# Activation transposes moved from TensorE to transposing DMAs in a decoder layer, and one projection folded into another

## The reference

```python
xn = rms_norm(h, norm_mix)
h = h + (g_a * (o_a @ w_br_gla) + g_b * (o_b @ w_br_dil)) @ w_mix_out
p = softmax(einsum('bshd,bmhd->bhsm', q, k) * X_HEAD_DIM ** -0.5)
h = h + einsum('bhsm,bmhd->bshd', p, v).reshape(b, s, D_MODEL) @ w_xo
```

## Time and profile before

| | us |
|---|---|
| median of 3 runs | 3063.55 (3058.01 to 3063.57) |
| profiled execution | 3062.74 |
| its span on the slowest core (the others from 3043.2) | 3061.2 |
| PE busy | 2918.9 |
| VectorE busy | 1843.2 |
| ScalarE busy | 1296.6 |
| GpSimd busy | 953.5 |

### The profile page before, as it was taken

The page is one execution under the profiler, slowest core; times in us unless marked ns, Lnnn a source line. Parts: engine busy times, 40 slices in busy tenths (PEclk is TensorE's granted clock), DMA queues, the critical chain, the costliest instruction groups (busy, mean ns, idle before and its releaser), DMA issues.

```text
span 3061.2 us, 55019 instructions; the slowest of 8 cores (3043.2 to 3061.2 us)
## 1 busy us (share of the span) xinstructions
PE 2918.9 (95%) x17454; PEld 1461.5 (48%) x17454; DVE 1843.2 (60%) x2994; ACT 1296.6 (42%) x2524; POOL 953.5 (31%) x1442
## 2 busy tenths in 40 slices
PE   5999999999999999899999989998999999999998
PEld 2444544555666554444444434444444444444443
DVE  4877766677766787344544346666644744754753
ACT  3666665566655666322232245665211211211211
POOL 1433333666776777233333210000200100100100
PEclk9999999999999999999999999999999999999999
DMA  6221103211221423644757395446811011011010
GB/s 145 72 73 50 55 28 80 61 50 40 55 65 43 100 78 84 138 132 150 188 147 167 107 192 176 159 148 193 165 56 64 20 56 69 15 55 69 15 55 28
DMA packets 96609, 278.99 MB, mean 91 GB/s; under 512 B 10920, under 2 KB 12228, under 8 KB 92868
## 3 DMA queue, kind: packets, MB, share of 16 engines
q1 hardware_dynamic: 81648, 223.91, 21.6%
q0 software_dynamic: 13568, 50.96, 10.8%
q10 hardware_dynamic: 1108, 0.60, 0.1%
HBM read 223.70 MB, written 102.63 MB: 107 GB/s over the span
## 4 chain that ended last, share of the span: by engine, by line
PE 78%; DVE 7%; ACT 6%; issue 5%; DMA 4%; DVEq 0%; ACTq 0%; POOL 0%; SPq 0%; POOLq 0%
PE psum L245 75%; PE psum L249 3%; ACT jh L271 1%; DMA wdn<-w_dn 1%; ACT junkX L271 1%; DVE on_112 L304 1%; ACT L271 1%; DMA x2i_220<-xn_d 0%; DMA oat<-oaT_d 0%; DVE cm_71 L308 0%; DMA h1x_234<-h_d 0%; DMA wvr_137<-w_gvr 0%; DMA grow_135<-gvec 0%; DVE x3s_246 L314 0%; DMA h1x_236<-h_d 0%
## 5 line engine op out<-in xcount | busy, mean ns | idle before, releaser
L245 PE MATMUL psum<-wd_140,xnT 128*128 128x512 bf16 x768 | 184.2, 385 | 7.8 <-DMA wd_140<-w_dil 7.8
L314 POOL COPY hist<-abt_278 128x2 f32<-128x2 f32 x88 | 17.4, 197 | 556.0 <-ACT abt_278 L313 556.0
L245 PE MATMUL psum<-wd_174,xnT 128*128 128x512 bf16 x768 | 185.4, 384 | 0.0
L245 PE MATMUL psum<-wd_175,xnT 128*128 128x512 bf16 x768 | 182.1, 380 | 0.0
L313 ACT COPY abt_278<-psum 128x512 f32<-128x512 f32 x88 | 50.2, 570 | 243.5 <-PE psum L245 243.5
L271 ACT ACTIVATE gl_276<-cv_0_272 128x512 f32<-128x512 f32 x88 | 55.5, 631 | 217.6 <-DVE cv_0_272 L304 217.6
L271 ACT ACTIVATE gl_277<-cv_1_273 128x512 f32<-128x512 f32 x88 | 55.5, 631 | 216.0 <-DVE cv_1_273 L304 216.0
L278 DVE TENSOR_TENSOR mab_197<-psum,sig_196 128x512 f32<-128x512 f32 x64 | 44.2, 691 | 146.2 <-PE psum L245 142.0
L245 PEld LDWEIGHTS psum<-wd_174,xnT 128*128 128x128 bf16 x768 | 103.0, 146 | 48.0
L278 DVE TENSOR_TENSOR qg_145<-psum,gqk 128x512 f32<-128x512 f32 x96 | 66.2, 689 | 90.0 <-ACT sq_142 L271 58.1
L278 DVE TENSOR_TENSOR qg_144<-psum,gqk 128x512 f32<-128x512 f32 x96 | 66.2, 690 | 89.1 <-ACT sq_142 L271 82.1
(11 more groups left out here) (748 smaller groups left out, 7821.0 us busy)
## 6 DMA issues: line engine op xcount, KB each, us to landing
ogl_176<-og_d SPq DMA_DIRECT2D x96, 260.0 KB, 4.9
og_d<-og_170 SPq DMA_DIRECT2D x32, 260.0 KB, 2.1
og_d<-og_171 SPq DMA_DIRECT2D x32, 260.0 KB, 2.1
og_d<-og_172 SPq DMA_DIRECT2D x32, 260.0 KB, 2.1
oaT_d<-oT_113 SPq DMA_DIRECT2D x32, 256.0 KB, 2.0
oat<-oaT_d SPq DMA_DIRECT2D x32, 256.0 KB, 4.3
xtT_203<-x SPq DMA_DIRECT2D x16, 512.0 KB, 7.3
h_d<-xtT_203 SPq DMA_DIRECT2D x16, 512.0 KB, 6.0
```

The costliest lines, as they stand in the source:

```text
L245: return self._add("pe", lambda e: e.matmul(o, l, r, start=start, stop=stop), [lhsT, rhs], [out], xr=xr)
L314: return self._add(eng, lambda e: e.tensor_copy(o, i), [in_], [out])
```

## The change

Transposing DMAs on SP (`dmat`, a new helper) take the place of `trans8` in `ntrans` from tile 8 on, `R_t`, `trans`, `og_trans`, `x2trans`, `q_trans` and `n_trans`. The keys of GLA, the memory and the first 8 input tiles stay on TensorE.

- The input tile is stored to DRAM (`xs_d`), and when a slab's four tiles are there, eight DMAs bring it back transposed, one for each 128 channels, each with a buffer record of its own. VectorE multiplies the gain in before (`gmb`, a broadcast load).
- The FFN's input is stored as it is, and four transposing loads bring a slab back (`x3_load`). The gain of the cross-attention's norm goes into the weights `wxq` on GpSimd (`kv_gx`).
- Orders move: in the GLA loop the values and scores of the next chunk come before `R_r`, and `P_za`, `P_z` after it; `trans` comes one step after the projections instead of two; `score`, `outp` and `x_out` come one iteration later, and the loop has one iteration more. `qkT` has four buffers. The copy of `va` goes from VectorE to ScalarE. Three slab loads wait for the last transpose of the dilated stage.
- The memory's values are made transposed (`kv_v`), multiplied once with the output projection (`kv_mx`, 32 matmuls), and `outp` is only a product of the probabilities with the inverse denominator; `x_out` multiplies them with the merged matrix.

```diff
+    def dmat(self, out, in_, xr=()):
+        o, i = out.ap, in_.ap
+        return self._add("sp", lambda e: e.dma_start_transpose(out=o, in_=i), [in_], [out], dma=True, xr=xr)
...
+            fw.stt("dve", xs[:, :], c["xt"][:, :], c["ss"][:, 2:3], gmb[:, :], ALU.mult, ALU.mult)
...
+        fw.dma(V(xs_d[i], xs_d[i].t[i * 128:(i + 1) * 128, :]), TCx[i]["xs"][:, :])
+        if i % 4 == 3:
...
+            for kc in range(8):
+                cs_ = slice(kc * 128, (kc + 1) * 128)
+                fw.dmat(V(xnk[s_][kc], xn[s_].t[:, kc, :]), V(xs_d[i - 3], xs_d[i].t[rows_, cs_]),
+                        xr=[V(xs_d[i - q], xs_d[i].t[rows_, cs_]) for q in range(3)])
...
     def R_t(c):
-        pt = trans8(PB.next(), cst_[c]["on"])
         oT = oTr.next()
-        fw.copy("act", oT[:, :, :], pt)
+        fw.dmat(oT[:, :, :], cst_[c]["on"][:, :])
         fw.dma(V(oaT_d[c], oaT_d[c].t[c]).rearrange("p (c t) -> p c t", c=8), oT[:, :, :])
...
-        pt = trans8(ptr_p, c["qkb"][:, :, :].rearrange("p a d -> p (a d)"))
         qkT = CC["qkTr"].next()
-        fw.copy("act", qkT[:, :, :], pt)
+        c["dT"] = fw.dmat(qkT[:, :, :], c["qkb"][:, :, :].rearrange("p a d -> p (a d)"))
...
         R_o(c)
-        if nx and c4 == 0:
-            P_za(s_ + 1)
         if nx:
             for h in ((), (0,), (1, 2), (3,))[c4]:
                 P_qk(s_ + 1, h)
         if c + 1 < NT:
-            R_r(c + 1)
-        if nx and c4 == 0:
-            P_z(s_ + 1)
+            R_v(c + 1, 0)
+            R_v(c + 1, 1)
+        if c + 1 < NT:
+            R_a(c + 1)
         if i < NT:
             nscale(i)
+            ntrans(i)
...
         R_on(c)
+        R_t(c)
...
         if c + 1 < NT:
-            R_v(c + 1, 0)
-            R_a(c + 1)
-            R_v(c + 1, 1)
+            R_r(c + 1)
+        if nx and c4 == 0:
+            P_za(s_ + 1)
+            P_z(s_ + 1)
...
+    def og_trans(i):
+        fw.dmat(ogc["obts"][i // 4 % 2][i % 4][:, :, :], TA[i]["obn"][:, :])
...
-        i, j, k = step, step - 2, step - 3
+        i, j, k = step, step - 1, step - 3
...
+    def kv_mx(h):
+        for mb in range(2):
+            for half in range(2):
+                cs_ = slice(half * 512, (half + 1) * 512)
+                p_ = PB.next()
+                for dc in range(2):
+                    fw.mm(p_[:, :], KV["VT"][:, 2 * h + dc, mb * 128:(mb + 1) * 128], KV["wxo"][h][:, dc, cs_],
+                          start=(dc == 0), stop=(dc == 1))
+                fw.copy("act", KV["MX"][h][:, mb, cs_], p_[:, :])
...
-        pt = trans8(PB.next(), qn)
-        fw.copy("dve", V(qTsub[s_ % 2][t_], qTs[s_ % 2].t[:, :, t_ * 128:(t_ + 1) * 128]), pt)
+        fw.dmat(qTsub[i // 4 % 2][i % 4][:, :, :], TC[i]["qn"][:, :])
...
+        fw.tt("dve", XL["pn"][s_ % 2][h][:, :, :], SC[s_][h][:, :, :], SC[s_]["rd"][:, :].raw(0, [[0, 2], [1, 512]]), ALU.mult)
...
+    def x3_load(s_):
+        for t_ in range(4):
+            i = s_ * 4 + t_
+            fw.dmat(F_["x3s"][t_][:, :, :], V(x3_d[i], x3_d[i].t[i]))
```

More of the change, by code:

```diff
@@ L509, in xn_reg @@
         for q in range(4):
-            xn[4 * hf + q] = b.sub("xn%d" % (4 * hf + q), xn_h[:, hf, :, q * 512:(q + 1) * 512])
+            s_ = 4 * hf + q
+            xn[s_] = b.sub("xn%d" % s_, xn_h[:, hf, :, q * 512:(q + 1) * 512])
+            if s_ >= 2:
+                xnk[s_] = [xn[s_]] + [b.sub("xn%d_%d" % (s_, kc), xn[s_].t) for kc in range(1, 8)]
+            else:
+                xnk[s_] = [xn[s_]] * 8
     xn_reg(0)
@@ L1081, in og_alloc @@
         ogc["ogl"] = r_.ring("ogl", 1, (128, 3, 520), F32)
-        ogc["obt"] = [r_.sb("obt%d" % q, (128, 4, 512), BF16) for q in range(2)]
+        ogc["obt"] = [r_.sb("obt%d" % q, (128, 4, 4, 128), BF16) for q in range(2)]
+        ogc["obts"] = [[b.sub("obt", b.t[:, t_]) for t_ in range(4)] for b in ogc["obt"]]
         ogc["rc"] = r_.ring("rcb", 2, (128, 8), F32)
@@ L1112, in og_div @@
         TA[i]["obn"] = obn
-    def og_trans(i, bank):
-        s_, t_ = i // 4, i % 4
-        ptb = bank[:, :].bitcast(BF16)
-        for cc in range(4):
-            fw.tr(ptb[:, cc * 128:(cc + 1) * 128], TA[i]["obn"][:, cc * 128:(cc + 1) * 128], ident_b)
-        obt = ogc["obt"][s_ % len(ogc["obt"])]
-        fw.copy("act", obt[:, :, t_ * 128:(t_ + 1) * 128], ptb[:, 0:512].rearrange("p (c t) -> p c t", c=4))
+    def og_trans(i):
+        fw.dmat(ogc["obts"][i // 4 % 2][i % 4][:, :, :], TA[i]["obn"][:, :])
     def oat_load(s_):
@@ L1153, in merge_br @@
             for kc in range(4):
-                fw.mm(py[:, :], sl[:, 16 + kc, :], ogc["obt"][s_ % 2][:, kc, :], start=(kc == 0), stop=(kc == 3))
+                ap = ogc["obt"][s_ % 2].t[:, :, kc, :]
+                ob = [V(b, ap) for b in ogc["obts"][s_ % 2]]
+                fw.mm(py[:, :], sl[:, 16 + kc, :], ob[0], start=(kc == 0), stop=(kc == 3), xr=ob[1:])
         ma = T1["ma"][br].next()
@@ L1208, in c_step @@
         if 0 <= t_ - 1 < 8 and ph == 1:
-            og_trans(t_ - 1, pj.next())
+            og_trans(t_ - 1)
         if 0 <= t_ < 8 and ph == 2:
@@ L1292, in kv_mm, with kv_v @@
         return p_
-    def kv_v(m):
-        for half in range(2):
-            p_ = kv_mm(m, half, True)
-            fw.copy("act", KV["Vm"][:, m, half * 512:(half + 1) * 512], p_[:, :])
+    def kv_v(q):
+        for c2 in range(2):
+            p_ = P.next()
+            for j in range(2):
+                c = q * 4 + c2 * 2 + j
+                for kc in range(8):
+                    fw.mm(p_[:, j * 256:(j + 1) * 256], KV["w"][:, kc, c * 128:(c + 1) * 128], KV["mn"][:, kc, :],
+                          start=(kc == 0), stop=(kc == 7))
+            c = q * 4 + c2 * 2
+            fw.copy("act", KV["VT"][:, c:c + 2, :], p_[:, :].rearrange("p (j n) -> p j n", j=2))
     def kv_k(m):
@@ L1329, in build @@
                (6, 1): [lambda: kv_v(1)], (6, 2): [kv_wxq]}
+    for q_ in range(4):
+        kv_plan[(7, q_)] = [lambda q_=q_: kv_gx(q_)]
     for s_ in range(NS):
@@ L1343, in build @@
                     if m > 0:
-                        og_trans(i - 1, P.next())
+                        og_trans(i - 1)
                 else:
@@ L1359, in build @@
             if 0 < s_ < NS - 1 and m == 7:
-                og_trans((s_ + 1) * 4 + 3, P.next())
+                og_trans((s_ + 1) * 4 + 3)
             for f_ in kv_plan.get((s_, m), ()):
@@ L1572, in build @@
     kv_wxo()
-    for k in range(NT + 11):
-        bg()
+    for k in range(NT + 12):
+        bg(2)
+        if 5 <= k < 9:
+            kv_mx(k - 5)
         if k < 5:
@@ L1579, in build @@
                 mix(NT - 4 + k)
-            x2trans(NT - 5 + k, PB.next())
+            x2trans(NT - 5 + k)
         if k == 5:
@@ L1620, in build @@
         if k >= NT + 5:
-            for _ in range(1 if k < NT + 9 else 2):
+            for _ in range(1 if k < NT + 10 else 2):
                 cur = up(0, len(UPD))
```

190 lines of the change are left out of this document (97 added, 93 removed).

## The result

The changed kernel takes 3137.59 us (median of four runs, 3135.5 to 3145.8) against 3062.85 for the kernel before: a ratio of 1.0252, 95% interval 1.0231 to 1.0274. The profiled execution has a span of 3134.0 us on its slowest core, 72.8 more than before. The forecast was 2998.

The account below looks back on a forecast made before the run. TensorE, busy 95%, was taken to bound the kernel. Gains of 43.2 (dilated), 5.8 (GLA) and 39.8 (cross-attention) less 23.8 (merge) took 65 us off 3062.7, giving 2998 us; range 2915 to 3045.

Parts of the forecast that it names:

- What left TensorE: Whole kernel: 2112 transposes (118.8 us) and a net 20.7 us of merged matmuls leave TensorE, 139.5 us if all stays hidden.
- X: Landing time of a 256 KB transposing DMA: bounded between 2.0 and 4.3 us, taken as 3.
- o: Spacing of the eight 128 KB slices replacing a group of input transposes: 0.32 to 4.1 us, taken as 1.15.
- upper bound of 130 ns a packet: Queue-line price per packet, giving 4.1 us as the upper end of the slice spacing.
- transposes are the bound: Rival: each 256 B piece costs a mean packet, 8.3 us per transpose; about 3460 us, cross-attention +90; chance 0.11.
- Dilated: Dilated stage, 96 items: DMA transposes stay hidden under 9.2 us of cover, each item 0.45 us shorter, gain 43.2 us.
- GLA: GLA stage: 25.1 us of transposes and 22.1 of waits go, six stalls behind slices add 41.4; net -5.8 us.
- The 22.1 us of waits on `on` and `vs`: GLA stage: PE's waits on `on` (12.0) and `vs` (10.1) go through the new order.
- Merge: Merge stage: 19.4 us of transposes go, six slab-boundary waits of 6.5 us plus 1.5 per restart add 43.2; net +23.8.
- Cross-attention: Cross-attention: 31.1 us of transposes and 20.7 of matmuls go, 12 given back where DMA is full; 8.2 us iterations, net -39.8.
- The rest: FFN input loads, slab loads, `wxq` scaling, constants and gain broadcast: covered or within the prologue, 0 us.
- 0.84 for faster: Chance of a faster kernel: 0.46 both stalls, 0.30 all or most hidden, 0.08 larger stalls.

Follow-up runs that it names:

- experiment 2: Changed kernel with input tiles from tile 8 transposed one by one from SBUF, no DRAM trip or slices: 3093.8 us on cores 0 to 3, against 3128.0.
- experiment 8: Changed kernel with all input-tile transposes back on TensorE, `R_t` still by DMA: 3098.9 to 3104.5 us, ratio 1.0129 to the kernel before.
- Experiment 1: Changed kernel with a slab's last dilated-output transpose issued ahead of that step's loads and store on SP: 3090.5 us on cores 0 to 3, against 3128.0.
- Experiment 3: Changed kernel with cross-attention's denominators after the query projection and query statistics before the residual's: 3107.7 us on cores 0 to 3, against 3128.0.
- experiment 5: Changed kernel with four extra, overwritten 512-column matmuls in each of 32 query projections: 3133.0 to 3137.7 us, ratio 1.0247 to the kernel before.
- experiment 4: Changed kernel with 13 `w_up` loads in cross-attention each waiting for its own iteration's query projection: 3102.7 us on cores 0 to 3, against 3128.0.
- experiment 7: Changed kernel with the last five mixer output norm tiles' transposes back on TensorE: 3111.3 to 3117.8 us, ratio 1.0170 to the kernel before.
- experiment 12: Changed kernel with edits of experiments 1 to 4, plus GLA's last four `R_t`, last five norm and first eight query transposes on TensorE: ratio 0.9778 to kernel before.
- experiment 6: Kernel before with only the dilated q/k transposes moved to DMA, one step after the projections, four buffers: 3035.2 to 3039.3 us, ratio 0.9921.

## Why the prediction was wrong

**What left TensorE.** Right: the page has 2176 fewer matmul instructions, as counted (2112 transposes, 96 matmuls, and 32 more of half width in `kv_v`).

**Price of the transposing DMA.** Right. X was taken as 3 us, and undisturbed landings are 2.7 to 3.1 us; o was taken as 1.15, and a slice takes 1.31. But o is not what the prediction reasoned it to be, time of the DMA engines by packets or bytes: they have a share of 0.40 while the slices go out (276.3 to 286.8 us), and a transposing DMA of twice the size holds SP for 1.22 to 1.24 us as well. What spaces the slices is the time that SP takes to issue one. The upper bound of 130 ns a packet is out: by SP's queue 285968 more packets took 35.8% of 3134.0 us in place of 21.6% of 3061.2 on 16 engines, an estimated 26 ns each. The Trainium skill's page "VectorE: DVE Perf Modes" (The three transpose paths) has 1309 ns for one 128x128 by DMA, by which eight would be an estimated 10.5 us: the trace does not agree, since eight in one DMA land after 3.1 at most. The Trainium skill's page "DMA: Bandwidth & Descriptors" (Latency and other measured facts) gives 261 GB/s, measured on one kernel, an estimated 0.5 us for a slice: a slice every 1.31 us is 100 GB/s, but as SP's issue sets that, no run here shows the page's figure or contradicts it. The rival "transposes are the bound", which hung on a price of 7 us, is out; it had the sign of the result and not its cause (its +90 for cross-attention does not follow from the terms printed beside it).

**Dilated, -43.2 forecast, -33.7 measured.** The mechanism was right: between 600 and 780 us PE has no idle time at all. The term was too large by the start of the pipeline, one wait of 4.8 us on the first `qkT`, and by 4.3 us of slower matmuls around it and around the wait on `w_dil`.

**GLA, -5.8 and +30.9.** The six stalls were put at 41.4 us together; measured are 30.0 on `za` and 11.4 on the slices, 41.4. The link to `on`, its buffer, VectorE and `za` is what the rows show, and experiments 2 and 8 confirm that the slices cause it. That `P_za` itself waits for the slices was overlooked; it only takes its share of the same stall, which `za` ends. That the sum agrees to the tenth is luck. Two steps failed. The 22.1 us of waits on `on` and `vs` that "go too" did not go on balance: all idle time apart from the stalls is 35.6 us, as before. Those on `vs` went, 16.5 us in this stage; in their place PE waits 11.8 on `R_o`'s bank behind `on` (8.7 on `on` itself before, in this stage), 6.7 on the state `U`, and 4.0 and 2.7 more on the weights `w_dil` and `w_gvr`. And the forecast charged restarts at the lower clock in the merge stage alone; here they cost 409.4 - (419.8 - 25.1) = 14.7 us.

**Merge, +23.8 and +29.9.** Right in place and cause, and in size on average: six waits of 6.95 us (3.1 to 10.5) instead of 6.5, restarts of 2.0 us instead of 1.5 (12.2 us of slower matmuls over six). Experiment 1 shows that the queue made nearly all of them.

**Cross-attention, -39.8 and +33.7.** This is the step that failed, 73.5 of the 138 us by which the sum was wrong, in three places.

- *The pace.* The forecast had 8.2 us an iteration, because ScalarE and VectorE "stay below that" with 6.3 and 6.8 of 10 us busy. Iterations 11 to 31 went from 10.23 only to 9.71. Busy time was the wrong reading: the two engines wait for each other in a closed chain of 9.7 to 10.0 us, and the code has that order before the change, too, under PE's 10.2. Experiment 3 cuts the chain and comes near the forecast's pace (8.42 us on average); experiment 5 shows 0.86 us of PE's work an iteration to be free under it. Of 20 x 2.0 = 40 us, 10 came.
- *The entry.* The forecast took 3 us for a query transpose that has "one whole iteration", gave back 12 us where the engines are full, and had no term for the transposes of the mixers' last five tiles, which fall here. k = 0 to 11 went from 101.2 to 133.0. Those transposes landed after up to 28 us beside 8.9 MB of weights; each is followed by a store, a load, a projection and a second transpose, on one queue. Experiments 4 and 7 show both sides: later weights give the whole 32 us back, and transposes on PE move the wait to the next transposing DMA. The kernel before had the same weights there and no transposing DMA, and took 101.2. No run tells how much is the lateness of a transpose and how much the store that holds SP until it has landed.
- *The end*, from k = 31 to the first up-projection, grew from 47.7 to 59.8 us: one iteration more, with waits of 7.4 on the last query transposes and 6.1 on the residual. That the pipeline became longer was not priced at all.

**The rest, 0 and +12.0**: 3.5 ahead of GLA, 8.5 in the FFN, where waits on `wdn` and `yT` grow by 3.9 and 5.4 us. No run takes these apart.

**The range** (to 3045) and the 0.84 for faster rested on cover being counted as an idle queue leaves it. "I would be wrong altogether if a transposing DMA slowed the plain traffic" came close: beside weights a plain DMA is as late as the transpose ahead of it on SP (experiment 7). But plain ones were late there before, too, so no run shows that the transposes are what slows them; that weight loads slow the transposes experiment 4 shows.

## What to carry to other kernels

Before work is taken from the busiest engine, walk round the loop with that engine left out, through every wait between the other engines: the loop can't run faster than the length of that closed chain, and it can't be read from busy shares. A transposing DMA is as good as its queue: price it where weights stream in, count the DMAs that wait for it on the same queue, put it ahead of loads that can wait, make it one DMA per tile, and keep the few that stand beside large loads on TensorE. And charge every new wait of TensorE twice, once for its length and once for the slow matmuls behind it (here 170 and 42 us).

## What the runs showed of the hardware

A transposing DMA of 256 KB lands after 2.7 to 3.1 us when little stands beside it, and much later beside large loads: after 6.8 and 20.4 us (medians), 28.1 at the worst, between 1780 and 1900 us. The stores of `xn_d` in the same stretch landed after 2.1 to 2.7, but that is no fair comparison: each goes out only when the transpose before it has landed. Where a plain DMA goes out right beside a late transpose it is as late: 30.7 and 34.4 us in experiment 7, where the transposes around them took 29.2 and 36.6; 20.2 for the load of `x2i` issued at 1868.71, 1.4 us behind a transpose that took 20.9; 20.3 in experiment 12 for the load of `h1x` at 1831.08, against 18.6. And in the kernel before, with the same weights and no transposing DMA, plain stores took 3.1 to 13.5 us and loads up to 19.7 in this stretch. So what these runs show is that a DMA beside large loads is late, transposing or not.

The issue is another matter. SP is held for 1.22 us by a transposing DMA on an idle queue and for 0.32 by a plain one. Where the engines are full, a transposing one held it for 11.16 us at 1874.34, for 23.22 in experiment 3 and for 25.00 in experiment 7. The two plain ones between the transposes of experiment 7 held it for 0.47 and 2.29, and the longest plain issue that the timelines up to 2300 us list by itself, in any of the runs, is one of 6.94 in experiment 6.

The packets are small: 292312 of 384132 are under 512 B, where before they were 10920 of 96609. Whether that is what holds the issue is not shown. The Trainium skill's page "Advanced Engine Details and Errata" (X-Bar Transpose (TRN2)) says that "TRN2 transpose DMAs are as fast as regular DMAs": with nothing beside them the rows come near that (3.1 us against medians of 2.1 for a store and 3.8 for a load of the same 256 KB), and beside weights the landings above agree with it.
